# Weighted values of the prompt's mLSTM on ScalarE instead of GpSimd, and fourteen unused matrix products in pairs 2 to 8

## The reference, cut to what matters

```python
m_new = jnp.maximum(b_end + m_st, jnp.max(dec, -1))
wk = jnp.exp(dec - m_new[..., None])
sc = jnp.exp(b_end + m_st - m_new)
c_new = sc[..., None, None] * c_st + jnp.einsum('bhl,blhe,blhd->bhed', wk, vc, kc)
n_new = sc[..., None] * n_st + jnp.einsum('bhl,blhd->bhd', wk, kc)
```

## Time and profile before

| | us |
|---|---|
| median of three runs | 909.11 |
| the three runs | 906.25, 909.11, 909.39 |
| the profiled execution | 902.73 |
| its span, first to last instruction | 901.0 |
| pair loop in it | about 281 to 440 |

### The profile page before, as it was taken

One profiled execution on the slowest core, in us unless ns is written; L12 is line 12 of the kernel. 1 busy time (PEld: TensorE's weight loads), 2 busy tenths in 40 slices (PEclk: granted clock), 3 DMA queues, 4 the chain that ended last, 5 costly groups with the idle time before them and its releaser, 6 DMA issues.

```text
span 901.0 us, 20128 instructions
## 1 busy us (share of the span) xinstructions
PE 845.1 (94%) x7849; PEld 767.3 (85%) x7849; DVE 580.4 (64%) x1208; ACT 417.4 (46%) x802; POOL 142.0 (16%) x260
## 2 busy tenths in 40 slices
PE   5999999899799898878999999999999999999994
PEld 5998888678788666646789999999999999999993
DVE  4633346541423589997578578888888888564655
ACT  5333255545523234486553466555555655221215
POOL 2012223443343200002000011111111111000000
PEclk9999999999999668899999999999999999999997
DMA  9267788979635000000323343222222222222222
GB/s 322 84 188 244 232 284 291 289 244 290 179 97 188 1 1 2 8 1 2 123 100 128 102 179 140 93 72 95 94 73 93 94 79 77 88 92 83 83 59 99
DMA packets 55009, 112.47 MB, mean 125 GB/s; under 512 B 7209, under 2 KB 32586, under 8 KB 54402
## 3 DMA queue, kind: packets, MB, share of 16 engines
q1 hardware_dynamic: 47074, 90.54, 30.3%
q0 software_dynamic: 6528, 17.83, 6.4%
q10 hardware_dynamic: 1312, 2.81, 1.1%
HBM read 105.54 MB, written 12.40 MB: 131 GB/s over the span
## 4 chain that ended last, share of the span: by engine, by line
PE 81%; DVE 8%; DMA 4%; issue 3%; ACT 3%; SPq 1%; POOLq 1%; ACTq 0%; POOL 0%; DVEq 0%
PE q L1998 32%; PE q L1996 30%; DMA arena<-in_pool 3%; PE q L2060 2%; DVE xt L1608 2%; PE q L2399 2%; PE q L2383 1%; PE q L2048 1%; PE q L2486 1%; PE q L2409 1%; DVE xt L1621 1%; PE q L2114 1%; PE q L2473 1%; PE q L2373 1%; PE q L2071 1%
## 5 line engine op out<-in xcount | busy, mean ns | idle before, releaser
L1996 PE MATMUL q<-arena_r,whi_r 128*128 128x256 f32 x672 | 199.4, 297 | 9.2 <-DVE wring_r L509 9.2
L1998 PE MATMUL q<-arena_r,whi_r 128*128 128x288 f32 (+1 forms) x672 | 200.3, 298 | 0.0
L1998 PE MATMUL q<-arena_r,wring_r 128*128 128x288 f32 (+1 forms) x672 | 200.1, 298 | 0.0
L506 ACT ACTIVATE whi_r<-wring 128x1024 fp32r<-128x1024 f32 (+1 forms) x99 | 102.3, 1033 | 206.1 <-PE q L1998 205.4
L509 DVE TENSOR_TENSOR wring_r<-wring,whi_r 128x1024 fp32r<-128x1024 f32 (+1 forms) x99 | 117.8, 1190 | 112.7 <-ACT whi_r L506 112.3
L1996 PE MATMUL q<-arena_r,wring_r 128*128 128x256 f32 x672 | 189.8, 283 | 0.0
L1998 PE MATMUL q<-xt_r,whi_r 128*128 128x290 f32 (+1 forms) x552 | 164.9, 299 | 0.0
L1996 PE MATMUL q<-xt_r,whi_r 128*128 128x256 f32 x552 | 155.8, 282 | 0.0
L1996 PEld LDWEIGHTS q<-arena_r,whi_r 128*128 128x128 f32 x672 | 128.0, 190 | 17.4 <-DVE wring_r L509 9.2
L1998 PEld LDWEIGHTS q<-arena_r,whi_r 128*128 128x128 f32 x672 | 128.1, 191 | 0.0
L1996 PEld LDWEIGHTS q<-arena_r,wring_r 128*128 128x128 f32 x672 | 128.0, 191 | 0.0
(11 more groups left out here) (483 smaller groups left out, 1616.4 us busy)
## 6 DMA issues: line engine op xcount, KB each, us to landing
wring<-in_w_up SPq DMA_DIRECT2D x42, 512.0 KB, 3.3
wring<-in_w_in SPq DMA_DIRECT2D x27, 512.0 KB, 5.4
arena<-in_pool SPq DMA_DIRECT2D x64, 192.0 KB, 4.0
arena<-in_pool POOLq DMA_DIRECT2D x64, 192.0 KB, 4.5
wring<-in_w_down SPq DMA_DIRECT2D x24, 448.0 KB, 3.4
wring<-in_w_out SPq DMA_DIRECT2D x8, 512.0 KB, 5.7
out_win_s<-in_win SPq DMA_DIRECT2D x8, 508.0 KB
arena<-in_pool SPq DMA_DIRECT2D x48, 64.0 KB, 2.3
```

What stands on the lines that cost most here:

```text
L506: return eng.activation(out, src, ACT.Copy)
L1996: pe.matmul(out[:, 0, 0:HALF], w, x[:, 0:HALF], start=(kk == 0 and n == 0), stop=(end and n == 2))
L1998: mm = pe.matmul(out[:, 1, 0:width - HALF], w, x[:, HALF:width], start=(kk == 0 and n == 0), stop=(end and n == 2))
```

## The change

GpSimd loses its four multiplications for `wv`. Its `masked_rows(2)` and `masked_rows(3)` stand alone and wait for the `exponents` alone.

ScalarE gets them as 32 ACTIVATE instructions of 128x65, a Copy with a scale from a column of `emp` for each head. The 8 of chunk 0 stand in pair 2, behind `probs(2)`. Those of chunks 1 to 3 stand behind `probs` in pairs 5 and 6, 9 and 10, 13 and 14, four in each.

TensorE gets two unused products of 512 columns in each of pairs 2 to 8, between `values_n(m - 3)` and `transposed(m - 2)`. They write to bank 4, whose last content has been copied out by then (the added wait is one that `values_n(m - 3)`, just ahead of it, has waited out already).

```diff
             def masked_rows(c):
                 if c >= 2:
                     pool.wait_ge(ml_d, c - 1)
-                    pool.wait_ge(ml_wv, c + 1)
...
-            pool.wait_ge(g_em, 1)
-            pool.wait_ge(prep, 3)
-            pool.wait_ge(tok_k_ev, 2 * (QT + 1))
-            pool.wait_ge(stored, 16 * 3)
-            for i in range(QT):
-                pool.wait_ge(tok_v_ev, i + 1)
-                pool.tensor_tensor(wv[:, i, :, :], tv[:, i, :, :], bc(emp[:, 64 + 8 * i:72 + 8 * i], HD + 1),
-                                   ALU.mult).then_inc(ml_wv, 1)
-                if i >= 2:
-                    masked_rows(i)
+            pool.wait_ge(prep, 4)
+            for c in range(2, QT):
+                masked_rows(c)
...
+            def weighted_values(c, heads):
+                act.wait_ge(tok_v_ev, c + 1)
+                if c == 0:
+                    act.wait_ge(prep, 3)
+                    act.wait_ge(g_em, 1)
+                    act.wait_ge(stored, 16 * 3)
+                for h in heads:
+                    ins = act.activation(wv[:, c, h, :], tv[:, c, h, :], ACT.Copy, scale=emp[:, 64 + 8 * c + h:65 + 8 * c + h])
+                if h == H - 1:
+                    ins.then_inc(ml_wv, 1)
...
                 if m < PAIRS:
                     probs(m)
+                if m == 2:
+                    weighted_values(0, range(H))
+                if 5 <= m < 4 * QT and m % 4 in (1, 2):
+                    weighted_values(m // 4, range(4 * (m % 4) - 4, 4 * (m % 4)))
...
                 if m >= LAG + 1:
                     values_n(m - LAG - 1)
+                if 2 <= m < 9:
+                    if m >= LAG + 1:
+                        pe.wait_ge(np_te, NG * (m - LAG - 1) + 1)
+                    unused_products(4, 2)
                 if LAG <= m < PAIRS + LAG:
                     transposed(m - LAG)
```

## The result

The changed kernel takes **917.9 us** (median of 20 runs, 905.6 to 930.8); the kernel before, run beside it, 909.2 us (20 runs, 904.0 to 918.5). The ratio is 1.0058 [1.0031, 1.0085]. The change makes the kernel slower. The forecast was 903.6 us, in a range of 900 to 912.5.

What follows compares the result with a forecast made beforehand. TensorE was taken to bound the kernel, at half clock early in the pair loop, VectorE later. Terms -0.5, +0.6, +2.1, -4.4, +1.0 gave -1.2; with -4.3 for the median, 909.11 became 903.6 us, range 900 to 912.5.

Steps and rivals of the forecast that it cites:

- What bounds the kernel: Whole kernel by TensorE; in the pair loop, TensorE at half clock for 30.6 us, then VectorE at full clock.
- The hole in pair 3: Before `states(0)`: eight ScalarE Copies in 2.2 us end the idle hole, cut from 3.6 to 3.1 us; -0.5 us.
- ScalarE in later pairs: Copies in pairs 5, 9, 13 cost nothing; in pair 10 they delay `states(2)`; +0.6 us, between 0 and 1.1.
- cover: VectorE's `logits(11)` and `gated(10)` hide part of the 1.1 us delay of `states(2)`; without it, 3.3 us.
- Products at the low clock: Pairs 3 and 4 at half clock: two unused products take 1.06 us in each pair; +2.1 us.
- What the products do to the clock: Clock rises around pair 4, so pairs 5 to 8 take 16.0 us instead of 20.4; -4.4 us.
- VectorE over 90% from there to pair 9: Sign of being right: VectorE this busy from the low stretch's end, by 312, to pair 9.
- the early rise: Clock back at full near 311 instead of 331.5, since two dense 512-column products stand in each pair.
- Products at the full clock: Eight products in pairs 5 to 8, 2.1 us, half hidden by VectorE's step; +1.0 us, between 0 and 2.1.
- From the profiled execution to the median: Low clock explains the runs' distance; an early clock rise removes two thirds of 6.4 us; -4.3 us.
- the products cost and bring nothing: Rival: twelve products delay TensorE in pairs 3 to 8 by 6.4 us; 915.6 us, chance 0.20.

Runs made afterwards that it cites:

- e10: The kernel before with 33 unused products placed in TensorE's idle holes of pairs 3, 7, 15 and 19; 903.6 us, ratio 0.9959.
- e1: The changed kernel without the unused products, leaving the weighted values by ScalarE alone; 913.4 us, ratio 1.0038.
- e8: The changed kernel without unused products, all eight ScalarE values of chunks 1 to 3 in pairs 5, 9 and 13; 910.5 us, ratio 1.0016.
- e2: The kernel before with the change's 14 unused products alone, weighted values still by GpSimd; 916.8 us, ratio 1.0075.
- e7: The kernel before with four unused products in each of pairs 2 to 8, 28 in all; 911.1 us, ratio 1.0046.
- e5: The kernel before with 13 unused products in TensorE's idle hole of pair 3 only; 905.7 us, ratio 0.9964.
- e11: The kernel before with two unused products in each of pairs 2 to 8, ahead of the mLSTM step; 911.3 us, ratio 1.0023.

## Why the prediction was wrong, point by point

**What bounds the kernel.** Right: the low stretch goes by TensorE, the rest of the loop by VectorE, as e10's 71 us show. What I missed is one step further: where VectorE sets the pace TensorE has holes, and in the changed kernel's trace each of the six falls in the loop follows a hole of 2.0 to 2.8 us. That low and full stretches feed each other in this way is my reading of that trace; the two holes of the kernel before with no fall behind them, and the falls without a hole below, say that it is not the whole of it. I treated the fall at 301 as one event with one end.

**The hole in pair 3.** Right. Forecast: eight Copies in 2.2 us, a hole of 3.1 us ended by ScalarE. Measured: 2.77 us, ended by line 1060 as the timeline above shows, and for the Copies

```profile
301.87 2.02 ACT L1060 ACTIVATE zt<-arena,emp 128x65 f32<-128x65 f32 x8
301.81 1.21 DVE L1640 TENSOR_TENSOR smem<-q,cst 128x1024 f32<-128x1024 f32 x1
```

VectorE's `decay(0)` ended at 303.02, 0.87 us ahead of ScalarE, as said ("some tenths to two us ahead"). `logits(0)` to `states(0)` took 17.7 us instead of 18.5, so there was a gain of 0.8 where I had 0.5; in e1, without products in the way, 17.2.

**ScalarE in later pairs.** The place was right, `states(2)` is released by ScalarE; the term (+0.6) was too small. The own cost of ScalarE's half was 1.4 ± 0.4 in e1 although it gains at `states(0)`, and e8 makes it likely that late values are its cause. The forecast said that ScalarE ending the waits of pairs 7 and 15 would prove its cover wrong: in the changed kernel's profiled execution VectorE ends both, but in e1 ScalarE ends both, after 1.46 and 1.98 us. So the cover that the +0.6 counted on was not safe. Something else was not in the sum at all: pair 11's hole went from 0.86 us to 1.98, and a low stretch began behind it, in which the pair took 8.3 us instead of 4.6. So 3.7 us were lost where the hole had grown by 1.1.

**Products at the low clock.** Right: +2.1 us forecast for pairs 3 and 4, measured 12.5 against 10.4.

**What the products do to the clock.** This is the step that failed, the term of -4.4. In the profiled execution the low stretch lasted 10.2 us, about as the forecast had it, and ended at 314.9 because the loop began 4 us later; but pairs 5 to 8 took 20.5 us as before, not 16.0. I multiplied the stretch that became faster and didn't ask what TensorE does there: at full clock it idled until pair 7's `states` for 2.47 us (0.58 before, hidden by its own slowness), and the clock fell again at 325. The check "VectorE over 90% from there to pair 9" shows it: 8.53 of 10.2 us is 84%, and then comes the fall. And e2's 34.0 us say that the rise itself was not secured by 14 products either. Over all runs the low time did not fall but rose (88 against 76), so in place of -4.4 the clock's term is about +4.6 by the fit.

The guess at the early rise also rested on two readings that the trace of the kernel before doesn't bear out. The low stretch of 3.5 us at 345.2 did not end behind wide products: the products in it have 128 columns, and the four of 256 of line 2399 begin at 348.62, when the clock was up again (at 348.5). And the pairs from 300.9 on do have wider ones than 128: the four of 512 columns of `exponents` at 316.46 and four of 256 at 326.26, and the clock stayed at 0.50 behind both, until 331.5.

```profile
326.26 1.23 PE L2399 MATMUL q<-zt 64*128 64x256 f32 x4
344.71 1.94 PE L2465 MATMUL q<-zt 64*128 64x128 f32 x14
346.58 1.12 PE L2383 MATMUL q<-whi,arena 128*64 128x128 f32 x8
347.63 1.06 PE L2409 MATMUL q<-cst,xt 128*128 128x128 f32 x4
348.62 0.70 PE L2399 MATMUL q<-zt 64*128 64x256 f32 x4
```

**Products at the full clock.** Half of them hidden was a guess, and the runs don't price this term by itself. With the one above it is +3.1 for the products; e2's own cost is 3.8 ± 0.4 (2.9 by the steeper slope), so the two together were about right. e7's 8.6 for twice as many says that more of them are not better hidden. They stood ahead of `transposed`, whose result ScalarE and then `states` and `values_n` want. My reason for hiding half was VectorE's longer step; but what VectorE does starts from results of this very chain.

**From the profiled execution to the median.** The mechanism was right, its sign was not. The runs of one kernel differ by their low time, as I had assumed from three runs without being able to see it. Each us of it costs 0.363 us, where the forecast had 4.4 in 20.4, or 0.22; the profiled execution before has 61 us of it where the mean is 76, which is 5.4 of the 6.4 us between it and the median. But the change did not remove it: the runs' spread grew from 14.5 to 25.2 us, and the profiled execution of the changed kernel lies below its median as well (916.98 to 917.9).

**The rival that came nearest** is "the products cost and bring nothing", 915.6 us at a chance of 0.20. By means of all runs the changed kernel stands 10.6 us above the runs of before that the line is fitted to (9.9 above the 20 beside it): 6.0 of own cost and 0.363 x 12.7 = 4.6 by 12.7 us more at the low clock. The forecast's rival had 6.4 us of it for the products and no clock term, so its nearness is in part luck. The forecast itself had -4.4 and -4.3 for the clock where the fit has +4.6, and +3.2 for all else (-0.5, +0.6, +2.1, +1.0) where it has +6.0. The Trainium skill's sentence on recent busyness (TensorE: Matmul & The Clock Gate, "What's actually happening") was weighed rightly against the row: in the windows after, too, the engine is busy 10.24 of 10.30 us and the clock reads 0.51. The same section has the idle engine fall back to the low clock; e5's filled hole, behind which the clock held until 311.9, fits that, but the fall at 345.2 before came without any idle time over 0.41 us on TensorE in the 4 us ahead, so idleness is not the whole of it.

**Open.** Why 14 products behind `values_n` raise the mean low time (88 ± 4; without them 76, doubled 63) isn't settled. There is one trace for each kernel, and the executions of one kernel differ by tens of microseconds of low clock, so I can't say which hole did it on average. Nor do I know why e11's own cost is above e2's. Nor is it settled whether filled holes keep the clock up because they are filled or because of the dense products in them; no run filled them with something else. And nothing in the change touches the work in which the 4.0 us before the loop were lost; in the profiled executions the low time there was 6.8 us before and 17.1 after.

## What to carry to other kernels

Ask of every stretch that a faster clock or engine would shorten what the engine behind the clock does in it: if another engine sets the pace there, new holes appear, and the clock may go again. Unused products belong into holes that already exist, sized to them (13 in 3.6 us cost 0.6 us), and not ahead of an instruction whose result someone waits for (about 0.3 us each). And take the mean clock of every run beside its time before you read a difference of one per cent out of two traces.

## What the runs showed of the hardware

- The scatter of this kernel from run to run, 901.7 to 920.9 us, is mostly time at the low clock: 0.363 us for each us of it, correlation 0.89. A stretch that goes by TensorE alone would give 0.5; VectorE's share in these stretches would explain less, which no run took apart.
- Low stretches of the loop were between 3.5 us and 40.9 us (e8, from 299.4) long, and the runs' mean clocks say that they differ from one execution of a kernel to the next.
- A hole of 2 to 3 us on TensorE was followed by a fall in six places of the changed kernel's trace, and not before at 377 and 411 or in e1 at 365. Over all thirteen traces, between 285 and 436 us, TensorE has 41 holes of 1.9 us or more that begin at the full clock; 29 have a fall in them or within 1.5 us behind them, 12 have not. And 17 of the 54 falls there come with no hole over 0.9 us in the 4 us ahead, as at 345.2 before and at 355.2 in e2, in both behind `cmp_scores`, products of 8 columns, and others of 128 and 256. I know of no rule from these runs that gets all of them.
- Eight Copies of 128x65 with a scale column took 2.02 us on ScalarE, 0.25 each, where the 128-element ones took 0.32.
- `gated` had its long instruction (1.15 us of a line whose shortest is 0.34) in the changed kernel too, though GpSimd's four multiplications are gone: `masked_rows(2)` ran beside it,

```profile
299.96 1.33 DVE L1628 TENSOR_SCALAR xt<-xt,gcol 128x128 f32<-128x128 f32 x2
300.12 2.18 POOL L782 TENSOR_TENSOR mixt<-gmx,cst 8x512 f32<-8x512 f32 x2 [15.36 <-PE q L2447]
```

as the forecast had refused to count on it. That the one stretches the other is read from their times only; no run took `masked_rows` away.
